# State space's output projection in four blocks of a row tile by 512 columns, keys channel-major, all latent probabilities divided in rows

## What is computed

```python
u_ssd, u_mla = split(rmsnorm(x) @ w_in)
# latent attention, 16 heads, 64 plain + 32 rotary channels, values of 64
q_lat, kv_lat, k_rope = split(u_mla, [384, 384 + 256])
q  = (rmsnorm(q_lat, q_norm_w) @ w_q_up).reshape(256, 16, 96)
kv = (rmsnorm(kv_lat, kv_norm_w) @ w_kv_up).reshape(256, 16, 128)
k_nope, v = split(kv, [64])
q_rope, k_rope = apply_rope(q[..., 64:]), apply_rope(k_rope)   # k_rope is shared by all heads
p = softmax((q_nope @ k_nope.T + q_rope @ k_rope.T) * 96**-0.5, masked by chunks of 64)
y_mla = p @ v
# state space: y_ssd, gated, normed in four groups of 256 channels
x = x + concat([y_ssd, y_mla]) @ w_out        # w_out: 2048 x 1024
```

## Time and profile before

| | us |
|---|---|
| median of 3 runs (lowest and highest) | 967.61 (967.47 to 967.87) |
| the profiled execution, device time | 967.69 |
| its span in the profile | 965.8 |
| PE busy | 955.4 |
| DVE busy | 639.3 |
| ACT busy | 516.0 |
| POOL busy | 80.6 |

### The profile page before, as it was taken

How to read it: one execution, slowest core, us unless ns; L and a number is a source line. 1 busy time by engine, 2 the same in 40 slices (tenths; PEclk the granted TensorE clock), 3 DMA queues, 4 the chain that set the end, 5 groups by cost and what they waited for, 6 DMA issues and landing times.

```text
span 965.8 us, 14530 instructions
## 1 busy us (share of the span) xinstructions
PE 955.4 (99%) x5515; PEld 823.8 (85%) x5515; DVE 639.3 (66%) x803; ACT 516.0 (53%) x748; POOL 80.6 (8%) x105
## 2 busy tenths in 40 slices
PE   9999999999999999999999999999999999999997
PEld 7888888887888888888889789889999899999996
DVE  5644544676665544546679798785666668777776
ACT  6444444466664344345657687555454475555544
POOL 4300000010110000000100923000000010000000
PEclk9999999999999999999999999999999999999999
DMA  9956556543347556556535253333653537465641
GB/s 308 305 185 196 193 174 207 185 142 142 99 159 244 174 188 195 181 180 212 182 131 185 84 173 103 126 131 134 224 188 109 174 102 240 145 212 172 204 144 44
DMA packets 110179, 166.04 MB, mean 172 GB/s; under 512 B 5748, under 2 KB 84884, under 8 KB 110004
## 3 DMA queue, kind: packets, MB, share of 16 engines
q1 hardware_dynamic: 108104, 160.45, 49.9%
q0 software_dynamic: 1872, 4.93, 1.6%
q10 hardware_dynamic: 160, 0.07, 0.0%
HBM read 164.38 MB, written 1.05 MB: 171 GB/s over the span
## 4 chain that ended last, share of the span: by engine, by line
PE 95%; ACT 2%; DVE 2%; DMA 1%; issue 0%; POOLq 0%; SPq 0%; POOL 0%
PE ps L2157 29%; PE ps L2159 28%; PE ps L2158 28%; PE ps L2442 1%; PE ps L2200 1%; PE ps L2897 1%; PE ps L2570 1%; PE ps L2181 1%; PE ps L2540 1%; DMA raw<-in_ffn_w_gu 1%; PE ps L2833 0%; ACT arena L923 0%; PE ps L2250 0%; PE ps L2251 0%; DVE arena L1697 0%
## 5 line engine op out<-in xcount | busy, mean ns | idle before, releaser
L1387 DVE TENSOR_TENSOR w_lo<-raw,w_hi 128x2048 fp32r<-128x2048 f32 (+2 forms) x142 | 321.6, 2274 | 138.0 <-ACT w_hi L635 137.9
L635 ACT ACTIVATE w_hi<-raw 128x2048 fp32r<-128x2048 f32 (+2 forms) x142 | 267.2, 1890 | 103.7 <-PE ps L2159 92.6
L2157 PE MATMUL ps<-w_hi,xT_hi 128*128 128x512 f32 (+2 forms) x722 | 276.9, 384 | 1.0 <-DVE w_lo L1399 0.8
L2159 PE MATMUL ps<-w_hi,xT_lo 128*128 128x512 f32 (+2 forms) x722 | 271.1, 375 | 0.0
L2158 PE MATMUL ps<-w_lo,xT_hi 128*128 128x512 f32 (+2 forms) x722 | 270.5, 375 | 0.0
L2157 PEld LDWEIGHTS ps<-w_hi,xT_hi 128*128 128x128 f32 x722 | 135.9, 188 | 26.0 <-issue 1.8
L2159 PEld LDWEIGHTS ps<-w_hi,xT_lo 128*128 128x128 f32 x722 | 135.8, 188 | 24.8
L2158 PEld LDWEIGHTS ps<-w_lo,xT_hi 128*128 128x128 f32 x722 | 136.1, 188 | 22.2
L2157 PE MATMUL ps<-xT_hi,w_hi 128*128 128x256 f32 x448 | 127.0, 284 | 0.0
L2159 PE MATMUL ps<-xT_hi,w_lo 128*128 128x256 f32 x448 | 126.8, 283 | 0.0
L2158 PE MATMUL ps<-xT_lo,w_hi 128*128 128x256 f32 x448 | 126.8, 283 | 0.0
(11 more groups left out here) (357 smaller groups left out, 1082.9 us busy)
## 6 DMA issues: line engine op xcount, KB each, us to landing
raw<-in_ffn_w_gu SPq DMA_DIRECT2D x84, 512.0 KB, 4.7
raw<-in_ffn_w_down SPq DMA_DIRECT2D x44, 512.0 KB, 3.9
raw<-in_w_ffn_up SPq DMA_DIRECT2D x44, 512.0 KB, 4.8
raw<-in_w_in SPq DMA_DIRECT2D x34, 512.0 KB, 4.6
raw<-in_w_out SPq DMA_DIRECT2D x24, 512.0 KB, 4.2
raw<-in_w_ffn_down SPq DMA_DIRECT2D x22, 512.0 KB, 4.2
raw<-in_w_mem_k SPq DMA_DIRECT2D x8, 512.0 KB, 3.9
raw<-in_w_mem_v SPq DMA_DIRECT2D x8, 512.0 KB, 4.3
```

The costliest lines, as they stand in the source:

```text
L635: act.activation(w_hi[HOME[k]][:, 0:n], raw[k % RING][:, 0:n], ACT.Copy).then_inc(rounded, 1)
L1387: TTn(w_lo[HOME[k]][:, 0:n], raw[k % RING][:, 0:n], w_hi[HOME[k]][:, 0:n].bitcast(F32), ALU.subtract).then_inc(resid, 1)
L2157: pe.matmul(out_, lh, rh, start=first, stop=False, **kw)
L2159: return pe.matmul(out_, ll, rh, start=False, stop=last, **kw)
```

## The change

- The output projection of the state space goes in four blocks of one row tile by 512 columns. A unit of weights now holds four row tiles of the weight by 512 columns, so a block needs two units (its two parts, 12 matmuls of 512 columns each into the whole of bank 7). DVE adds each block by itself. The fourth unit's rest is made in two halves.
- The keys come out of the projection with channels on partitions. DVE scales the latent keys by their row's factor before PE turns them (`kv_scaled`); POOL makes that factor earlier. The two `kvup` units are reordered while they are split, keys of eight heads ahead of their values, by two instructions each on ACT and on DVE. The keys need no turning: ACT copies those of even heads, DVE those of odd heads from PSUM (64 partitions by 1024 elements) to `kT2`. The rotary part of the key is turned once (two transposes), copied by ACT and spread over the other 15 heads by a DMA from ACT's queue. POOL's spreading copies go.
- Two of POOL's four rotary products of the queries move to DVE.
- `norm("out_ssd")` stands ahead of the heads and waits for the copies of the keys (`kv_act`, `kv_dve`). Only the queries are turned by heads.
- In the last group the probabilities are divided in rows as in the others; the turning of the factors goes. `scaled_input("mk")` moves behind the last group's result.

```diff
@@ sync @@
                 if i == 3:
                     sp.wait_ge(scaled, SCALE_FIRST.index("out_ssd") + 1)
+                    sp.wait_ge(kv_ps, 1)
...
-                load(k, rows_by_cols(k, a["w_out_2"][0], 0, 8, 256 * i, 256))
+                load(k, rows_by_cols(k, a["w_out_2"][0], 4 * (i % 2), 4, 512 * (i // 2), 512))
@@ scalar @@
+                if isinstance(c, int) and U0["kvup"] <= k < U0["out_ssd"]:
+                    for r in range(2):
+                        last = act.activation(kv_parts(w_hi[HOME[k]], r), kv_sorted(raw[k % RING], k, r), ACT.Copy)
...
+            act.wait_ge(kv_ps, 1)
+            act.activation(kT2[NOPE:QK, 0, :], ps[NOPE:QK, 7, 0:S], ACT.Copy).then_inc(kv_act, 1)
+            act.wait_ge(kv_act, 1)
+            act.dma_start(kT2[NOPE:QK, 1:MH, :],
+                          kT2[NOPE:QK, 0:1, :].broadcast_to([ROPE, MH - 1, S])).then_inc(k_rope_spread, 16)
+            split(U0["kvup"] + 2)
+            for i in range(2):
+                act.wait_ge(kv_ps, i + 2)
+                act.activation(kT2[0:NOPE, 8 * i:8 * i + 8:2, :], k_tiles(0, i), ACT.Copy).then_inc(kv_act, 1)
+                if i == 0:
+                    split(U0["kvup"] + 3)
+                act.wait_ge(unit_used, U0["kvup"] + i + 1)
+                act.activation(v_tok[:, 0, 512 * i:512 * i + 512], ps[:, 4 * i + 2, :], ACT.Copy).then_inc(kv_act, 1)
@@ gpsimd @@
-            for i in range(4, 8):
+            step_rows(4)
+            norm("mla")
+            for i in range(5, 8):
                 step_rows(i)
             skip(1)
-            norm("mla")
             norm("out_ssd")
...
-            for v, x_, i in ((t4[0], h1, 1), (t4[1], h2, 0), (t4[2], h2, 1), (t4[3], h1, 0)):
+            for v, x_, i in ((t4[0], h1, 1), (t4[1], h2, 0)):
                 last = TTp(v, x_, both(i), ALU.mult)
             last.then_inc(rope2_parts, 1)
-            pool.wait_ge(rope2_parts, 1)
+            pool.wait_ge(rope2_parts, 2)
@@ vector @@
             decay_mask(5)
+            rstd_is("mla")
+            for t in range(TT):
+                scale_rows(tail[:, t, T_KV:T_KV + KVR], tail[:, t, T_KV:T_KV + KVR],
+                           rstd_mla[:, t, 1:2]).then_inc(kv_scaled, 1)
             dve.wait_ge(off_ps, 1)
...
+            scaled_input("out_ssd")
...
+            keys_odd(0)
+            split(U0["out_ssd"])
+            values_1(0)
...
+            dve.wait_ge(q2_act, 3)
+            dve.wait_ge(q2_dve, 3)
+            TTn(rope_tmp[2][:, :, :, :], q2, both(1), ALU.mult)
+            TTn(rope_tmp[3][:, :, :, :], q1, both(0), ALU.mult).then_inc(rope2_parts, 1)
+            split(U0["out_ssd"] + 1)
+            keys_odd(1)
+            values_1(1)
+            dve.wait_ge(rope2_parts, 2)
+            TTn(q2, rope_tmp[2][:, :, :, :], rope_tmp[3][:, :, :, :], ALU.add).then_inc(rope2_done, 1)
+            for j in range(1, 8, 2):
...
             row_max(0)
-            split(U0["out_ssd"] + 1)
             side_add(0)
...
-                if gi < 3:
+                if gi == 1:
+                    split_halves(U0["out_ssd"] + 3)
+                elif gi < 3:
                     split(U0["out_ssd"] + gi + 2)
-                if gi == 2:
-                    scaled_input("mk")
...
+                if gi == 3:
+                    scaled_input("mk")
@@ tensor @@
             pe.wait_ge(off_read, 1)
+            pe.wait_ge(kv_scaled, TT)
             norm("mla")
...
+            for t in range(TT):
+                last = pe.transpose(ps[0:QK, 7, t * P:t * P + P], tail[:, t, T_KR - NOPE:T_KR + ROPE], ident)
+            last.then_inc(kv_ps, 1)
+            for i in range(2):
+                k = U0["kvup"] + i
                 pe.wait_ge(resid, k + 1)
...
+                for q in range(4):
+                    for r in range(2):
+                        last = product(ps[:, 4 * i + q // 2, q % 2 * S:q % 2 * S + S], wt(k, 1024 * r + P * q, P),
+                                       (xT_hi[:, 3 + r, :], xT_lo[:, 3 + r, :]), r == 0 and q % 2 == 0, r == 1,
+                                       skip_group_check=True)
+                last.then_inc(kv_ps, 1)
...
+            pe.wait_ge(kv_act, 4)
+            pe.wait_ge(kv_dve, 3)
+            norm("out_ssd", 0, 6)
+            pe.wait_ge(kv_act, 5)
+            norm("out_ssd", 6, 2)
+            pe.wait_ge(rope2_done, 2)
             for j in range(8):
                 turn_heads(j)
-            norm("out_ssd")
-            pe.wait_ge(rope2_done, 2)
-            for j in range(8, 16):
-                turn_heads(j)
...
-            turn_factors(3)
             turn_probs(3)
```

More of the change, by code:

```diff
@@ L1110, in _ @@
                     split(U0["kvup"] + i)
[L1111 to L1122, removed]
+            act.wait_ge(kv_ps, 1)
[11 more added lines that the diff above has]
+                act.activation(v_tok[:, 0, 512 * i:512 * i + 512], ps[:, 4 * i + 2, :], ACT.Copy).then_inc(kv_act, 1)
+            for j in range(0, 8, 2):
                 act.wait_ge(mT_ps, j + 1)
-                dst = kT2 if j < 8 else qT2
-                act.activation(dst[0:QK, 2 * (j % 8):2 * (j % 8) + 2, :],
+                act.activation(qT2[0:QK, 2 * j:2 * j + 2, :],
                                ps[0:QK, MT_BANK[j % 4], :].rearrange("p (a b) -> p a b", a=2), ACT.Copy).then_inc(mT_act, 1)
@@ L1691, in attn_factors @@
                 link(nc.vector.reciprocal(rec[:, gi % 2, :, :], p_sum[:, gi % 2, :, :]))
-                if gi < 3:
[L1693 to L1702, removed]
+                at = 0
+                for t in range(TT):
+                    n = nk[t] * P
+                    v = prob(gi)[:, at:at + hg * n].rearrange("p (h n) -> p h n", h=hg)
+                    last = TTn(v, v, bc(rec[:, gi % 2, t, :], n), ALU.mult)
+                    at += hg * n
+                last.then_inc(rec_ready, 1)
             def attn_out(gi):
@@ L1997, in _, with keys_odd @@
[L1997 to L2001 removed]
+            scaled_input("out_ssd")
+            def keys_odd(i):
+                dve.wait_ge(kv_ps, i + 2)
+                nc.vector.tensor_copy(kT2[0:NOPE, 8 * i + 1:8 * i + 8:2, :], k_tiles(1, i)).then_inc(kv_dve, 1)
@@ L2543, in turn_probs @@
                 last.then_inc(pT_ps, 1)
-            def turn_factors(gi):
-                pe.wait_ge(rec_ready, gi + 1)
-                if gi:
-                    pe.wait_ge(o_ready, gi)
-                for pair in range(2):
-                    for t in range(TT):
-                        at = pair * S + t * P
-                        last = pe.transpose(ps[:, 6, at:at + P], o2T[:, 2 * gi + t, pair * P:pair * P + P], ident)
-                last.then_inc(recT_ps, 1)
             def weighted(gi):
@@ L2573, in weighted, with out_ssd @@
                 last.then_inc(o_ps, 1)
-            def out_ssd(i, t, between=None):
-                k = U0["out_ssd"] + i
-                if t == 0:
-                    pe.wait_ge(resid, k + 1)
-                    if i:
-                        pe.wait_ge(side_added, i)
-                for r in range(KT):
-                    if i == 0 and t == 0:
-                        xT_there("out_ssd", r)
-                    if r == 4 and between is not None:
-                        between()
-                    last = product(ps[:, 7, t * 256:t * 256 + 256], xT(r, t), wt(k, 256 * r, 256), r == 0, r == KT - 1)
-                if t == 1:
+            def out_ssd(i, part):
+                h, t = i // 2, i % 2
+                k = U0["out_ssd"] + 2 * h + part
+                if i == 2 and part:
+                    pe.wait_ge(first_resid, 6)
+                else:
+                    pe.wait_ge(resid, k + 1)
+                if part == 0 and i == 3:
+                    pe.wait_ge(x_ready, 2 * XU.index("out_ssd") + 1)
+                elif part == 0 and i:
+                    pe.wait_ge(side_added, i)
+                for r in range(4):
+                    if i == 0:
+                        xT_there("out_ssd", 4 * part + r)
+                    if i == 2 and part and r == 2:
+                        pe.wait_ge(resid, k + 1)
+                    last = product(ps[:, 7, :], xT(4 * part + r, t), wt(k, 512 * r, 512), part == 0 and r == 0,
+                                   part == 1 and r == 3)
+                if t:
                     last.then_inc(unit_used, 1)
+                elif part:
+                    last.then_inc(side_ps, 1)
             pe.wait_ge(half_ready, 1)
```

144 lines of the change are left out of this document (65 added, 79 removed).

## The result

The changed kernel takes 971.58 us, the median of 5 runs (971.52 to 972.73), against 967.61 us: 1.0044 times the time before, 95% interval 1.0033 to 1.0055. It is slower by 0.4%. I had forecast 968.5 us (965.5 to 971.5), no change that can be told.

What follows compares the result with a forecast made beforehand. PE was taken as the bound, busy 955.4 of 965.8 us. +2.3 us at the heads' end and -1.5 for groups, first division and last group gave +0.8 on 967.69: 968.5 us, range 965.5 to 971.5.

Steps and rivals of the forecast that it cites:

- Where PE would wait, and for what: Ahead of the state space input's 16 transposes, PE waits 4.1 us (3.6 to 4.7) for DVE's second odd-key copy.
- The size of DVE's row: DVE's instructions from POOL's factor for the state space's input to the second odd-key copy: 10.8 to 11.8, taken as 11.3 us.
- two products for the rotary part, new on DVE, 0.6 each: In DVE's row before the second odd-key copy, the two query rotary products moved from POOL, 0.6 us each.
- the whole meeting with POOL: Lengthening of DVE's row where two of its instructions meet POOL's: the sum of 10.8 us taken as 11.3.
- x: Delay before the query projection's first product, from scaling latent keys before PE turns them: 1.0 us, between 0.45 and 2.1.
- rival (b): PE's long wait halves its clock for the transposes behind it: 0 to 5.5 us, 2.7 taken, 971.2 us; chance 0.16.
- Key/value projection: On PE, 48 matmuls of 256 plus 24 of 512 columns, switches and two transposes: 0.84 us longer.
- Groups: In the groups of heads, six output-projection parts on PE fall to 2.83 to 2.87 us each: 0.93 us saved.
- The 0.15 for an earlier first division: DVE's addition ahead of the groups comes earlier, which starts the first division earlier: 0.15 us saved.
- No gain ahead of the groups: The two projection parts ahead of the groups, 5.9 us then 5.55, save nothing because PE already waits for ACT's exponentials.
- Last group: From the projection's end to the weighted sums' end, 3.70 us becomes 3.3: 0.4 us saved.

Runs made afterwards that it cites:

- keys first: Changed kernel with DVE's copies of the second half of the odd keys and of the values ahead of the second projection-unit split: 969.70 us.
- the split put back: The reordered kernel with its first state-space split put back ahead of DVE's copy of the second half of the odd keys: 967.06 us.
- the reordered kernel: Changed kernel with latent-key scalings ahead of the last decay mask, DVE's copies ahead of both splits, six of eight query copies on ACT: 965.52 us.
- the filled wait: Changed kernel with five unused fp32 matmuls of 512 columns added on PE in front of its wait: 970.16 us.
- the POOL products cut: Changed kernel with POOL's two rotary products cut to one head of the 16 in each row tile: 970.11 us.

## Why the prediction was wrong

- **Where PE would wait, and for what: right.** The wait stands ahead of the 16 transposes, behind DVE's copy of 64 x 1024, with the row in the order I gave; keys first, the split put back and the reordered kernel confirm it.
- **The size of DVE's row: the step that failed first.** I said 10.8 to 11.8 us and took 11.3; it took 12.5 (578.74 to 591.26). From start to start all its terms held within 0.15 us but one: "two products for the rotary part, new on DVE, 0.6 each", which took 2.69 with POOL's products beside them. I had allowed 0.5 us for the whole meeting with POOL, taken from a split that was lengthened by 0.65. I had weighed the rule of the shared ports for x, and not for the two instructions that the change itself puts beside POOL's. The copy thus ended 1.1 us later behind x than forecast, and PE came 0.25 us sooner: the wait was 5.4 us, not 4.1.
- **The clock: not in the forecast, but in rival (b)**, at 0.16. Its price was 0 to 5.5 us and 2.7 taken; it cost 1.33 in the trace, and 1.42 in the median by the filled wait. Its upper end, all transposes at half speed, did not come: the clock was back at 1.00 by 595 us with nothing but transposes on PE. Its bound was wrong: the one gap that the trace of before had, 4.3 us at its end, was an upper bound for the length from which the clock falls, and I used it as the length itself. It fell with a wait of 3.90 us too, so the 4.1 us of my forecast would most likely not have kept it. That this rival's 971.2 us lies 0.4 from the measured 971.58 is luck: its wait of 4.1 and clock of 2.7 add up to 6.8 us, and so do the measured 5.5 and 1.3.
- **x: 1.27 us for 1.0**, inside 0.45 to 2.1. But POOL's skip product met the decay mask, not the scalings.
- **Key/value projection: +0.63 for +0.84.** Too careful by 0.2.
- **Groups: -0.68 for -0.93.** Twelve matmuls at 0.2275 are 2.73 us; the parts took 2.94 and 2.86 in the mean. A switch thus costs 0.13 to 0.2, where I put 0.1. The 0.15 for an earlier first division did not come: the saving of the first group is 0.26 us, little more than the others' 0.23 and 0.19.
- **No gain ahead of the groups: right** (5.08 us late at the first scores and at the second). **Last group: -0.38 for -0.4**, right.

Together: +2.8 us at the first scores (wait 1.4, clock 1.3, x and projection 0.1), and +0.4 after it.

## What to carry to other kernels

Where PE is full, work taken off it counts only if no other engine's row becomes the last: write that row down instruction by instruction, and where a two-input instruction may lie beside POOL's, give it both prices (here 0.6 us for a product alone, 1.0 and 1.7 beside POOL). A long wait of PE can cost its clock as well: 1.4 us on top of the 5.4 here, and next to nothing on top of 3.15, where the next work waited for another engine anyway. Work on DVE that nobody waits for yet (here two splits) belongs behind the copies that PE waits for. That order, with the scalings ahead of the mask and two of DVE's copies on ACT, turned the change from 4.0 us slower into 2.2 us faster; one split put back ahead cost 1.5 of it.

## What the hardware showed that I had not expected

- The granted clock fell to half with waits of PE of 3.08, 3.15, 3.17, 3.90, 5.38 and 5.39 us, and not with 2.31, 1.53, 1.07 and 0.60 us in the traced executions. The fall can also come when the wait is already over: with the POOL products cut, PE was back at 589.78 us, and the clock was still 1.00 until 590 and fell in the microsecond behind it (mean 0.72). Once PE was back, it did nothing but transposes at half clock, and the clock came back under them (594 to 595 us in the kernel after).
- A product of 128 x 32 elements on POOL took 3.40 us with DVE's split beside it, and 128 x 512 took 1.28 us while DVE read PSUM: beside DVE's splits the length of a POOL instruction says little of its size.
- DVE's copy of 64 x 1024 elements from PSUM took 1.23 us with POOL busy beside it, as in the forecast, and its copy of 128 x 512 took 0.69 us beside POOL's product (584.42 in the kernel after) and 0.69 with POOL idle (591.29): these reads of PSUM were not lengthened.
